# MLA attention steps: half of the second gate product is carried into the next step, and the steps' side work is put in another order

## The reference

```python
u = rmsnorm(h, pre_norm_g)
proj = u @ w_in            # cq, ckv, k_pe, z_mla, fq, fk, fv, f_logit, z_fox, gates
q  = rmsnorm(cq) @ w_uq    # 16 heads, 64 plain + 32 rotary features each
kv = rmsnorm(ckv) @ w_ukv  # 16 heads, 64 of keys + 64 of values
q_m = concat(q_nope, rope(q_pe));  k_m = concat(k_nope, rope(k_pe))
o_mla = causal_block_attention(q_m, k_m, v_mla, MLA_SCALE)
y_mla = (o_mla * silu(z_mla)) @ w_br_mla
o_fox = causal_block_attention(fq, fk, fv, FOX_SCALE, cumulative forget gate)
y_fox = (o_fox * silu(z_fox)) @ w_br_fox
mixed = (sigmoid(gate_a) * y_mla + sigmoid(gate_b) * y_fox) @ w_out
```

## Time and profile before

| | |
|---|---|
| median of three runs | 1834.51 us |
| the profiled execution | 1835.31 us, span 1833.6 us |
| PE busy | 97% of the span |
| DVE, ACT, POOL busy | 50%, 42%, 20% |
| chain that ended last | PE 89%, DVE 5%, ACT 3% |
| mean granted PE clock | 0.992 |
| MLA steps 1 to 7 | 70.83 to 295.29 us of the span |

### The profile page before, as it was taken

The page is one execution under the profiler, slowest core; times in us unless marked ns, Lnnn a source line. Parts: engine busy times, 40 slices in busy tenths (PEclk is TensorE's granted clock), DMA queues, the critical chain, the costliest instruction groups (busy, mean ns, idle before and its releaser), DMA issues.

```text
span 1833.6 us, 25452 instructions
## 1 busy us (share of the span) xinstructions
PE 1774.6 (97%) x8811; PEld 1470.5 (80%) x8811; DVE 922.1 (50%) x1461; ACT 765.1 (42%) x1333; POOL 359.3 (20%) x390
## 2 busy tenths in 40 slices
PE   6999999999999999979999999999999999999998
PEld 5777778898987888858878888888888788888886
DVE  4556565565655333377455555533336555555332
ACT  5556566554554223333343333322264443333222
POOL 4434435433321000130021111101002211111000
PEclk9999999999999999989999999999999999999999
DMA  4211112212122333313323333333332233333332
GB/s 118 63 43 38 51 44 52 55 48 58 47 57 61 100 92 114 117 54 90 102 86 100 92 92 99 93 118 94 95 96 70 82 104 92 96 99 92 95 95 86
DMA packets 282519, 150.13 MB, mean 82 GB/s; under 512 B 11791, under 2 KB 278034, under 8 KB 282450
## 3 DMA queue, kind: packets, MB, share of 16 engines
q1 hardware_dynamic: 281874, 148.95, 28.1%
q0 software_dynamic: 544, 0.20, 0.1%
q10 hardware_dynamic: 32, 0.07, 0.0%
HBM read 147.02 MB, written 2.16 MB: 81 GB/s over the span
## 4 chain that ended last, share of the span: by engine, by line
PE 89%; DVE 5%; ACT 3%; issue 1%; POOL 1%; SPq 1%; DMA 0%; DVEq 0%; ACTq 0%; POOLq 0%
PE ps L331 68%; PE ps L888 5%; PE ps L768 3%; PE ps L2196 2%; PE ps L745 2%; PE ps L727 2%; PE ps L734 1%; PE ps L774 1%; PE ps L781 1%; PE ps L629 1%; ACT w_split L291 1%; DVE w_split L302 1%; DVE arena_r L1185 1%; DVE big L1771 0%; DVE arena_r L1155 0%
## 5 line engine op out<-in xcount | busy, mean ns | idle before, releaser
L331 PE MATMUL ps<-u,w_split 128*128 128x512 f32 x3888 | 928.3, 397 | 15.6 <-DVE u L1776 8.4
L331 PEld LDWEIGHTS ps<-u,w_split 128*128 128x128 f32 x3888 | 727.7, 189 | 183.8 <-issue 11.3
L302 DVE TENSOR_TENSOR w_split<-w_raw,w_split 128x1024 fp32r<-128x1024 f32 (+1 forms) x221 | 268.1, 1213 | 435.6 <-ACT w_split L291 435.6
L291 ACT CAST w_split<-w_raw 128x1024 fp32r<-128x1024 f32 (+4 forms) x321 | 288.6, 913 | 415.3 <-PE ps L331 380.7
L331 PE MATMUL ps<-arena_r,w_split 128*128 128x512 f32 x1824 | 417.4, 390 | 1.7 <-DVE arena_r L2336 1.7
L331 PEld LDWEIGHTS ps<-arena_r,w_split 128*128 128x128 f32 x1824 | 341.8, 188 | 74.4 <-DVE arena_r L2336 3.2
L302 POOL TENSOR_TENSOR w_split<-w_raw,w_split 128x1024 fp32r<-128x1024 f32 (+3 forms) x100 | 136.5, 1383 | 51.6 <-ACT w_split L291 39.6
L2116 POOL TENSOR_TENSOR tmp<-tmp 128x512 f32<-128x512 f32 x44 | 56.9, 1294 | 424.8 <-ACT tmp L2101 424.8
L954 ACT ACTIVATE tmp<-ps,stats 128x144 f32<-128x144 f32 (+3 forms) x128 | 69.3, 541 | 144.8 <-DVE stats L1142 144.3
L1625 POOL TENSOR_TENSOR tmp<-tmp 128x512 f32<-128x512 f32 x40 | 56.8, 1421 | 269.5 <-ACT tmp L1584 234.5
L888 PE MATMUL ps<-u,w_split 128*128 128x264 f32 x768 | 104.4, 288 | 0.5 <-POOL w_split L302 0.5
(11 more groups left out here) (249 smaller groups left out, 1542.7 us busy)
## 6 DMA issues: line engine op xcount, KB each, us to landing
w_raw<-in_w_in_dram SPq DMA_DIRECT2D x118, 256.0 KB, 3.2
w_raw<-in_w_ffn_gate_dram SPq DMA_DIRECT2D x88, 256.0 KB, 3.1
w_raw<-in_w_ffn_up_dram SPq DMA_DIRECT2D x88, 256.0 KB, 3.1
w_raw<-in_w_ffn_down_dram SPq DMA_DIRECT2D x64, 256.0 KB, 3.1
w_raw<-in_w_in_even_dram SPq DMA_DIRECT2D x32, 256.0 KB, 3.1
w_raw<-in_w_in_odd_dram SPq DMA_DIRECT2D x32, 256.0 KB, 3.2
w_raw<-in_w_ffn_down_dram SPq DMA_DIRECT2D x32, 192.0 KB, 2.7
w_raw<-in_w_br_mla_dram SPq DMA_DIRECT2D x16, 256.0 KB, 3.1
```

Of the source, the lines that this page charges most:

```text
L291: ins = act.copy(dst, src)
L302: ins = dve.tensor_tensor(lo, r, hi, ALU.subtract)
L331: last = pe.matmul(out_ap, w_tile(c, ws, k - n0), moving(k, ms), start=start and n == 0, stop=stop and n == len(total) - 1, skip_group_che ...
```

## The change

Four things are moved, and no product, copy or split is added or dropped.

- The second gate product z_fox is cut after its fourth k tile. The first half stays at the end of its step (slots 6 and 7), the second half, 12 matmuls, becomes `z_carried` in slot 0 of the next step, behind the first scores and ahead of the keys' product. Its copy out of PSUM (`act_z`) and the hi split of unit c+1, which waits for it, follow in slot 0 of ACT.
- On PE the rotary queries move from slot 0 to 1, the plain queries from 1 to 2, the values from 2 to 3, and z_mla starts with one k tile in slot 3.
- On DVE the keys' lo split moves ahead, from slot 2 to 1, where the rotation was; the rotation moves to 2, the queries' lo split from 3 to 4, the values' from 5 to 6.
- On ACT the keys' hi part stays in slot 1; the queries' hi part moves from 2 to 3, the rotary copy from 3 to 4, the values' from 4 to 5, the hi split of unit c+2 from 3 to 4. On POOL the rotation's sum moves from 2 to 3, the rope's lo parts from 4 to 5, the lo split of unit c+2 from 3 to 4.

Step 0 makes only the first half of its z_fox; step 8, the first fox step, takes over the last carried half. The waits on `z_read` are adapted.

```diff
+        def z_carried(pe, s, c):
+
+            b = 7 if isinstance(s, int) and s == 1 else 0
+            product(pe, bank(b), c - 1, u_real, (4, 5, 6, 7), start=False).then_inc(sem("w_used"), 1)
...
-                    pe.wait_ge(sem("z_read"), 2 * s)
+                    pe.wait_ge(sem("z_read"), 2 * s - 1)
...
             def q_nope():
+                if later:
+                    pe.wait_ge(sem("z_read"), 2 * s)
                 mla_q(pe, 0, qkv, 0).then_inc(sem("qn_done"), 1)
...
-                        lambda: (q_rope(), q_nope()), lambda: (k_and_meta(), v()), lambda: z(7, zf, range(KT))]
+                        lambda: (q_rope(), q_nope()), lambda: (k_and_meta(), v()), lambda: z(7, zf, (0, 1, 2, 3))]
 
             def first():
+                z_carried(pe, s, c)
                 k_and_meta()
-                q_rope()
+
+            def middle():
+                v()
+                z_mla(0)
 
             def turn():
-                z_mla(6, 7)
+                z_mla(7)
                 z_fox(0)
 
-            return [first, q_nope, v, lambda: z_mla(0, 1, 2), lambda: z_mla(3, 4, 5), turn,
-                    lambda: z_fox(1, 2, 3), lambda: z_fox(4, 5, 6, 7)]
+            return [first, q_rope, q_nope, middle, lambda: z_mla(1, 2, 3), lambda: z_mla(4, 5, 6), turn,
+                    lambda: z_fox(1, 2, 3)]
...
             def part(b):
+                if b == 0 and isinstance(s, int) and s == PAIRS:
+                    z_carried(pe, s, c)
...
+        def act_z_carried(act, s, c, kk, i):
+
+            act_z(act, s - 1 + PAIRS, 7 if isinstance(s, int) and s == 1 else 0, c - 1, kk, i)
...
-                elif b in (0, 3):
-                    w_hi(act, c + (1 if b == 0 else 2), i, kk, "full")
+                elif b == 0:
+                    if gemm == "mla" or (isinstance(s, int) and s == PAIRS):
+                        act_z_carried(act, s, c, kk, i)
+                    w_hi(act, c + 1, i, kk, "full")
+                elif b == (4 if gemm == "mla" else 3):
+                    w_hi(act, c + 2, i, kk, "full")
                 if gemm == "mla":
                     if b == 1:
                         act_k(act, s, c, gemm, par, kk, i)
-                    elif b == 2:
+                    elif b == 3:
                         act_q(act, s, c, gemm, par, kk, i)
-                    elif b == 3:
+                    elif b == 4:
                         act_rope(act, s, par)
-                    elif b == 4:
+                    elif b == 5:
                         act_v(act, s, c, gemm, par, kk, i)
...
                 if gemm == "mla":
                     if b == 1:
+                        dve_k(dve, s, gemm, par, 0)
+                    elif b == 2:
                         dve_rotate(dve, s, 0)
-                    elif b == 2:
-                        dve_k(dve, s, gemm, par, 0)
-                    elif b == 3:
+                    elif b == 4:
                         dve_q(dve, s, gemm, par, 0)
-                    elif b == 5:
+                    elif b == 6:
                         dve_v(dve, s, gemm, par, (0,))
```

More of the change, by code:

```diff
@@ L876, in feature @@
                             pe.wait_ge(sem("v_split"), s)
-                            pe.wait_ge(sem("z_read"), 2 * s)
                     elif j == 1:
                         pe.wait_ge(sem("v_split"), s)
+                        if isinstance(s, int) and s == PAIRS:
+                            pe.wait_ge(sem("z_read"), 2 * s)
                     else:
@@ L1083, in act_first @@
             w_hi(act, nxt)
-            act_z(act, PAIRS, 7, c + 2)
         def act_step(act, s, attn, gemm, par, c, kk=0, i=0, nxt=None):
@@ L1123, in act_step @@
             act_p(act, pr, 7)
+            if gemm == "mla" and par:
+                act.wait_ge(sem("z_read"), 2 * s + 1)
             act.wait_ge(sem("pm_transposed"), pr + 1)
@@ L1128, in act_step @@
             if gemm == "mla":
-                if par:
-                    act.wait_ge(sem("z_read"), 2 * s + 1)
-                act_z(act, s + PAIRS, 0, c + 2, kk, i)
                 if par:
@@ L1258, in dve_step @@
                     if b == 1:
+                        dve_k(dve, s, gemm, par, 1)
+                    elif b == 2:
                         dve_rotate(dve, s, 1)
-                    elif b == 2:
-                        dve_k(dve, s, gemm, par, 1)
-                    elif b == 3:
+                    elif b == 4:
                         dve_q(dve, s, gemm, par, 1)
-                    elif b == 5:
+                    elif b == 6:
                         dve_v(dve, s, gemm, par, (1, 2))
@@ L1345, in pool_step @@
                 if gemm == "mla":
-                    if b == 2:
-                        pool.wait_ge(sem("pm_copied"), 8 * pr + 2)
+                    if b == 3:
+                        pool.wait_ge(sem("pm_copied"), 8 * pr + 3)
                         pool_rotate(pool, s)
-                    elif b == 4:
+                    elif b == 5:
                         pool.wait_ge(sem("w_lo"), num(c, i, kk) + 3)
@@ L1355, in pool_step @@
                         w_lo(pool, MIX + (1 if b == 0 else 2))
-                elif b in (0, 3):
-                    w_lo(pool, c + (1 if b == 0 else 2), i, kk, "full")
+                elif b == 0:
+                    w_lo(pool, c + 1, i, kk, "full")
+                elif b == (4 if gemm == "mla" else 3):
+                    w_lo(pool, c + 2, i, kk, "full")
                 elif b == 6:
```

## The result

The changed kernel takes 1872.01 us (four runs, 1871.01 to 1873.23) against 1835.06 of the kernel before: ratio 1.0196, 95% interval 1.0183 to 1.0209. It is slower by 37 us; 1862.0 was forecast. The profiled execution took 1872.95 us with a span of 1871.3. No time or ratio in this document counts one execution of experiment 5, which took 4514.06 us against 1856 to 1857 of the other three.

The account below looks back on a forecast made before the run. PE was busy 97% of the span, so time is lost only where it waits or runs at half clock. 1835.3 + 21.9 (steps) + 5.6 (clock) - 0.8 = 1862.0 us; range 1844 to 1875, own range 1852 to 1869.

Parts of the forecast that it names:

- Start of a step: Slot 0 of an MLA step: scores 1 start at t = 4.39 us behind carried product; table load covered.
- The keys ahead on DVE: DVE in slot 1 waits for ACT's key copies: block lo split 2.05 us later, scores 3 at t = 11.43.
- Rotation and values: Rotation's second half on DVE ends at t = 12.76; PE waits 0.3 us for it at the values' product.
- Slots 3 to 6: ACT and DVE, not PE, set the time: scores 7 at t = 24.64, 1.2 us more of waits.
- The clock: One half-clock PE stretch in each of seven MLA steps, 0.8 us each: +5.6 us, bounds 1.4 and 12.
- The sum: MLA steps 2 to 7 +17.9 us, step 1 +1.2, step 8 +2.83: together +21.9, before the clock's +5.6.
- Rival C of the prediction: Port collision or clock hits every step: 7 to 14 us more, 1869 to 1876 and over; chance 0.09.
- The port rule: GpSimd's exclusive lock might hold DVE's normalisation 5 up to 1.0 us; taken as 0, as a rival 1.0 a step.
- Rival A: Only the front costs, ACT's slots 4 to 6 have slack: step 1.7 us longer, 1844 to 1846; chance 0.17.
- Rival B: Keys' hi part is ready for DVE, waits of 5.0 and 3.2 us go: 1825 us; chance 0.05.
- Rival D: Over the whole kernel the waits only change names: 1834.5 us; chance 0.03.

Follow-up runs that it names:

- experiment 5: Changed kernel with ACT's copy of the keys' hi part also moved ahead, from slot 1 to the end of slot 0: 1856.72 us, ratio 1.0115.
- experiment 1: Changed kernel with DVE's old order back, rotation in slot 1 and keys' lo split in slot 2: 1850.61 us, ratio 1.0079.
- experiment 4: Changed kernel without the carrying, z_fox finished in its own step, all other moves kept: 1870.14 us, ratio 1.0179.
- experiment 3: Kernel before with the carried half product alone, ACT, DVE and POOL in their old order: 1852.04 us, ratio 1.008.
- experiment 2: Changed kernel with the plain queries' product done twice in MLA steps 1 to 7, 10 us more matmuls: 1864.62 us, ratio 1.0149.
- Experiment 6: The kernel of experiment 1 with ACT's copy of the plain queries moved from slot 3 to 2 as well: 1846.23 us, ratio 1.0057.
- experiment 7: Kernel before with both halves of the rotation on DVE ahead of the normalisation of block 1: ratio 0.9996.
- experiment 8: Kernel before with the first gate product waiting only for the first half of the keys' lo split: ratio 0.9995.

## Why the prediction was right, and where it was off

**Start of a step**: scores 1 at t = 4.32 (4.39 worked out). The load of the exp table behind a Silu is still there (1.28 us, at 182.01 in step 4) but costs nothing: scores 3 of step 4 start at t = 11.33, as in step 3.

**The keys ahead on DVE**: right in each part. DVE idles 2.07 us for ACT's copies, the lo split comes 2.05 later (5.49 - 3.44), transposes wait 1.66, scores 3 another 0.70 and start at t = 11.35 (11.43 worked out). Experiments 1, 4 and 5 show it as the largest cause; experiment 3 shows that carrying costs as well.

**Rotation and values**: 0.2 of wait (0.3), product at t = 12.74 (12.8).

**Slots 3 to 6**: scores 7 at t = 26.56 instead of 24.64; but in the step of experiment 2 at full clock they start at 24.57 and the step is 34.72 long against 34.86, so the chain was right and the difference is the clock. Experiment 6 shows the chain.

**The clock**: this is the term that was mis-sized. One stretch of 3.4 us a step was forecast, costing 0.8; there were stretches of 6.8 us in five of the seven steps, two of 3.4 in step 1 and one of 3.4 in step 5, costing 2.0 a step by the estimate above, 14.2 instead of 5.6 and over the stated bound of 12. The stretch of step 3 begins at 156.3, behind two idles of 1.66 and 0.70 that lie within 2.8 us, and ends at 163.2. I had priced it from step 2 of before, where later waits absorbed it; here the matmuls, twice as long, held up ACT's copy of block 2 and with it the whole chain behind (the copy waited 1.99 us for the transposes, and not at all in step 2 of experiment 2). A single stretch of 3.4 us made a step longer by 0.6 (experiment 1, step 5), 1.1 (experiment 7, step 5), 1.3 (changed kernel, step 5) and 1.5 (experiment 6, steps 3 and 4), so 0.8 was low but near; what failed more is their number.

**The sum**: all but the clock +20.3 measured, +21.9 forecast; clock 14.2 for 5.6; and 3.2 behind step 8 where nothing was forecast. So the forecast fell 10 us short because the clock cost 8.6 more and the 3.2 came on top, while the chain cost 1.6 less. Step 8 grew by 2.8, as forecast; step 1 began at 69.76 where 70.35 was forecast.

**Rival C of the prediction.** At 1872 the time lies outside the forecast's own range of 1852 to 1869 and inside that of this rival (0.09), 1869 to 1876. Its clock half is what came true in size. Its place did not: the additional half-clock time is in one longer stretch behind the waits at the front of a step, and not in second stretches behind the waits at scores 7. That the whole range, up to 1875, holds the measured time is owed to the allowance made for this rival.

**The port rule** of the Trainium skill (SBUF — State Buffer, Who interferes with whom) as a rival had 1.0 a step. The normalisation of block 5 did come beside the rope's lo parts on GpSimd, but only in one step of seven was it held, as these rows of DVE and POOL in the changed step 4 show:

```profile
204.90 1.44 DVE L1170 TENSOR_SCALAR tmp<-tmp,stats 128x272 f32<-128x272 f32 x1
```

```profile
203.53 2.66 POOL L1313 TENSOR_TENSOR arena_r<-tmp,arena_r 32x512 fp32r<-32x512 f32 x2
```

It ended 0.15 after GpSimd's pair of instructions, which agrees with the rule, and this step is the longest of steps 2 to 7. In the other six it took 0.36 (step 3: 168.34, with the pair at 167.11 to 169.86), so 1.1 us in all and not 7. The held one started 1.37 after the pair's start, the six others 1.23 to 1.25 after; why this decides, the rows do not show, since they give the pair as one. The 1.46 us of the earlier trace rows did not recur in slot 1, as forecast.

**Rival A** (the second half has slack) is out by experiment 6 and the steps of 34.7. **Rival B** is out by the sign, and experiments 7 and 8 say why its arithmetic fails: in the odd steps a PE wait was worth nothing while the block chain over DVE and ACT ended at the same time as before. In the even steps of experiment 7 the wait of 1.5 us, with the clock behind it, was worth 1.1 and 1.4.

**Rival D** (all cancels) is out by the sign as well.

## What to carry to other kernels

When side work is moved a slot ahead, move it on every engine that it passes through: here one engine's split was put in front of the common chain while the copy that feeds it stayed behind, and the chain paid for it. Before pricing a wait at its length, ask what PE meets next: two waits of 5.0 and 3.2 us were removed one at a time for no gain that the runs could tell, and together, with a shorter ACT chain, for 7 us. Price twice the idle that a change adds, once for itself and once for the clock that falls behind it.

## What was not expected of the hardware

In these kernels half-clock time went with idle that is bunched more than with its sum. Experiments 3 and 5 both have 3.4 us of waits in a step such as step 2. In experiment 3 they are 0.3 to 0.9 long, with 1.7 us and more between any two, and no step had a stretch at half clock. In experiment 5 three of them (0.71, 0.70 and 0.3) lie within 3.2 us, and each of steps 4 to 7 had 3.4 or 6.8 us. With 1.66 and 0.70 close together five steps of seven had 6.8.

It is not a matter of the waits of a step alone, though. Steps 2 and 3 of experiment 5 had no half clock, with the same three waits; in experiment 7 step 5 had 3.4 us and step 3 none, with equal waits. What decides between them, these runs do not show, so an estimate of the clock needs a wide range. Adding 10 us of matmuls into the 1.66 us gaps made the changed kernel some 9 us faster.
